# One decoder block on one core: z tiles with meta tokens as two products of 264 columns, one sum of squares over 528 columns, and another order at the start

## The reference, cut to what matters

```
h = concatenate([meta_tokens, x])            # (528, 1024)
y = h * rsqrt(mean(h * h, axis=-1) + 1e-6) * mix_norm_g
z = y @ w_in                                 # 4864 columns: recurrence (q, f, v, gate), attention (q, k, v), branch gates
```

## Time and profile before

| what | us |
|---|---|
| median of 3 runs (1732.18 to 1735.71) | 1732.32 |
| the profiled execution's own time | 1731.5 |
| its span, first to last instruction | 1729.4 |
| PE busy, share of the span | 97% |
| DVE busy | 72% |
| ACT busy | 40% |
| POOL busy | 36% |

### The profile page before, as it was taken

The page is one execution under the profiler, slowest core; times in us unless marked ns, Lnnn a source line. Parts: engine busy times, 40 slices in busy tenths (PEclk is TensorE's granted clock), DMA queues, the critical chain, the costliest instruction groups (busy, mean ns, idle before and its releaser), DMA issues.

```text
span 1729.4 us, 24964 instructions
## 1 busy us (share of the span) xinstructions
PE 1681.4 (97%) x9279; PEld 1477.5 (85%) x9279; DVE 1243.9 (72%) x2191; ACT 688.2 (40%) x978; POOL 628.1 (36%) x420
## 2 busy tenths in 40 slices
PE   7999999999999999999999999999999999999997
PEld 4788866777889999999999999999999999998886
DVE  2550468581688979996877777777777777777875
ACT  4322244543333447775333333333333333333333
POOL 3656233445334542221543343333333333332210
PEclk9999999999999999999999999999999999999999
DMA  3222111143222336678988888888888888888873
GB/s 117 81 73 97 38 49 49 57 151 110 76 83 82 126 122 198 211 208 270 345 304 311 314 298 320 306 293 326 303 301 313 305 316 298 315 278 297 314 258 121
DMA packets 140950, 364.83 MB, mean 211 GB/s; under 512 B 10576, under 2 KB 59728, under 8 KB 140880
## 3 DMA queue, kind: packets, MB, share of 16 engines
q1 hardware_dynamic: 54000, 201.96, 32.7%
q0 software_dynamic: 36864, 134.23, 22.5%
q10 hardware_dynamic: 50016, 27.79, 5.4%
HBM read 336.68 MB, written 27.26 MB: 210 GB/s over the span
## 4 chain that ended last, share of the span: by engine, by line
PE 77%; DVE 14%; issue 3%; ACT 2%; POOL 2%; DMA 1%; SPq 0%; POOLq 0%; ACTq 0%; DVEq 0%
PE ps L1213 71%; DVE hot_g L1150 3%; DVE hot_g L1153 3%; DVE hot_i L1151 3%; PE ps L1279 2%; PE ps L1338 1%; DVE orstd L951 1%; DMA raw<-in_wstream 1%; ACT atp L588 1%; DVE o_hg L952 1%; PE ps L1538 1%; POOL wlo L413 0%; DVE atstat L923 0%; DVE atsc L919 0%; PE ps L1240 0%
## 5 line engine op out<-in xcount | busy, mean ns | idle before, releaser
L1213 PE MATMUL ps<-hThi,uwhi 128*128 128x384 f32 x1024 | 348.6, 340 | 1.8 <-DVE uwlo L1092 1.5
L1213 PE MATMUL ps<-hThi,uwlo 128*128 128x384 f32 x1024 | 344.0, 336 | 0.0
L1213 PE MATMUL ps<-hTlo,uwhi 128*128 128x384 f32 x1024 | 343.1, 335 | 0.0
L1213 PE MATMUL ps<-vwhi,awhi 128*128 128x512 f32 x768 | 299.7, 390 | 3.0 <-DVE awlo L1112 3.0
L1213 PE MATMUL ps<-vwlo,awhi 128*128 128x512 f32 x768 | 299.9, 390 | 0.0
L1213 PE MATMUL ps<-vwhi,awlo 128*128 128x512 f32 x768 | 299.4, 390 | 0.0
L1097 DVE TENSOR_TENSOR vwlo<-vraw,vwhi 128x1024 fp32r<-128x1024 f32 x128 | 156.8, 1225 | 174.5 <-ACT vwhi L719 174.4
L413 POOL TENSOR_TENSOR wlo<-raw,whi 128x1024 fp32r<-128x1024 f32 x66 | 163.4, 2476 | 297.3 <-ACT whi L505 297.3
L719 ACT ACTIVATE vwhi<-vraw 128x1024 fp32r<-128x1024 f32 x128 | 135.8, 1061 | 336.0 <-PE ps L1213 311.3
L468 POOL DMA_INDIRECT rows<-in_u,gidx x128 | 166.6, 1302 | 267.5 <-DVE rows L1120 248.9
L468 POOL DMA_INDIRECT rows<-in_v,gidx x128 | 145.5, 1137 | 297.0 <-DVE acc L1127 279.4
(11 more groups left out here) (292 smaller groups left out, 2820.5 us busy)
## 6 DMA issues: line engine op xcount, KB each, us to landing
uraw<-in_uT SPq DMA_DIRECT2D x128, 512.0 KB, 4.6
vraw<-in_v SPq DMA_DIRECT2D x128, 512.0 KB, 4.7
raw<-in_wstream SPq DMA_DIRECT2D x72, 512.0 KB, 3.2
gates_dram<-piece ACTq DMA_DIRECT2D x12, 2048.0 KB, 9.4
gmat<-gates_dram SPq DMA_DIRECT2D x32, 768.0 KB, 7.6
xt<-in_xT SPq DMA_DIRECT2D x8, 264.0 KB, 6.4
acc<-in_x ACTq DMA_DIRECT2D x1, 2048.0 KB, 11.2
rows<-in_u,gidx POOLq DMA_INDIRECT x128, 6.0
```

Source lines behind the costliest of these rows:

```text
L1213: ins = pe.matmul(dst, lhs[a], rhs[b], start=first and i == 0, stop=last and i == 2)
```

## The change

Tiles with meta tokens become 48 products of 264 columns (two halves of the 528 tokens in two PSUM banks), with the same stationary weights for both halves; the separate meta products, `znat`, its copies and `turn_meta` go. The squares are made after all of y, DVE adds the 8 chunks, and PE multiplies the one sum by ones (2 products of 264 columns) after tile 1. Root and reciprocal are taken over 528 columns. At the start the first 256 columns of tile 0's weights are loaded first and by themselves, then `xt` chunk 0, and `sinks` last; a small ACT copy stands ahead of everything. POOL splits tile 2's weights before it waits for `rstd`, and tile 3's after the scale of tile 0. v and av of the meta tokens are turned in the transposing steps, of which there are 12, with 2 gate products each.

```diff
-TURNED = 10
+TURNED = 12
+SPAN = LEN // 2
+EARLY = 2 * P
...
-            sp.dma_start(par[:], params).then_inc(S["par_in"], 16)
-            sp.dma_start(sink[:], sinks.to_broadcast([P, AQ])).then_inc(S["par_in"], 16)
-            sp.dma_start(raw[:, 0, :], wstream[0]).then_inc(w_in[0], 16)
-            for c in range(DC):
+            sp.dma_start(raw[:, 0, 0:EARLY], wstream[0, :, 0:EARLY]).then_inc(S["early_in"], 16)
+            sp.dma_start(xt[:, 0, :], xT[:, 0, :]).then_inc(xt_in[0], 16)
+            sp.dma_start(par[:], params).then_inc(S["par_in"], 16)
+            sp.dma_start(raw[:, 0, EARLY:D], wstream[0, :, EARLY:D]).then_inc(w_in[0], 16)
+            for c in range(1, DC):
                 sp.dma_start(xt[:, c, :], xT[:, c, :]).then_inc(xt_in[c], 16)
-                if c == 1:
-                    sp.dma_start(raw[:, c, :], wstream[c]).then_inc(w_in[c], 16)
+                if c == 3:
+                    sp.dma_start(raw[:, 1, :], wstream[1]).then_inc(w_in[1], 16)
+            sp.dma_start(sink[:], sinks.to_broadcast([P, AQ])).then_inc(S["sink_in"], 16)
...
+            split_lo(2, 0, slot(0))
             pool.wait_ge(S["rstd_ok"], 1)
-            scale_blocks(0, 4, zm[:, :, META:LEN], 0, "z_copied", "z_out")
+            for k in range(2):
+                if k == 1:
+                    split_lo(3, 1, slot(1))
+                pool.wait_ge(S["z_copied"], k + 1)
+                own = zm[:, k:k + 1, :]
+                pool.tensor_tensor(own, own, rstd[:].unsqueeze(1), ALU.mult).then_inc(S["z_out"], 1)
+            scale_blocks(2, 4, zm, 0, "z_copied", "z_out")
...
+            act.wait_ge(poo, 1)
+            act.activation(rstd[:, 0:1], eps[:], ACT.Copy)
+            act.wait_ge(S["early_in"], 16)
+            act.activation(w["hi"][:, 0, 0:EARLY], raw[:, 0, 0:EARLY], ACT.Copy).then_inc(S["early_hi"], 1)
+            act.wait_ge(S["par_in"], 16)
             for c in range(DC):
                 act.wait_ge(xt_in[c], 16)
                 act.activation(y["hi"][:, c, :], xt[:, c, :], ACT.Copy, scale=mix_g[:, c:c + 1]).then_inc(S["yhi_ok"], 1)
+                if c == 0:
+                    act.wait_ge(w_in[0], 16)
+                    act.activation(w["hi"][:, 0, EARLY:D], raw[:, 0, EARLY:D], ACT.Copy).then_inc(S["w_hi"], 1)
+                if c == 3:
+                    split_hi(1, 1)
+            for c in range(DC):
                 act.activation(xsq[:, c, :], xt[:, c, :], ACT.Square).then_inc(S["xsq_ok"], 1)
+            act.wait_ge(S["w_used"], 1)
+            act.activation(spans(zm[:, 0]), ps[:, 0:2, 0:SPAN], ACT.Copy).then_inc(S["z_copied"], 1)
+            split_hi(2, 0)
+            act.wait_ge(S["w_used"], 2)
+            act.activation(spans(zm[:, 1]), ps[:, 4:6, 0:SPAN], ACT.Copy).then_inc(S["z_copied"], 1)
+            split_hi(3, 1)
             act.wait_ge(S["xsum_ok"], 1)
-            act.activation(sd[:], ps[:, 4, :], ACT.Sqrt, bias=eps[:], scale=1.0 / D).then_inc(S["sd_ok"], 1)
+            act.activation(spans(sd[:]), ps[:, 6:8, 0:SPAN], ACT.Sqrt, bias=eps[:], scale=1.0 / D).then_inc(S["sd_ok"], 1)
...
+            for c in range(1, DC):
+                dve.wait_ge(S["xsq_ok"], c + 1)
+                need(dve, S["xadd_ok"], c - 1)
+                dve.tensor_tensor(xsq[:, 0, :], xsq[:, 0, :], xsq[:, c, :], ALU.add).then_inc(S["xadd_ok"], 1)
...
+            def with_meta(k, c):
+                for i, (a, b) in enumerate(SPLIT):
+                    for n, own in enumerate(halves):
+                        ins = pe.matmul(ps[:, 4 * k + n, 0:SPAN], w[a][:, k, c * P:(c + 1) * P], y[b][:, c, own],
+                                        start=c == 0 and i == 0, stop=c == DC - 1 and i == 2)
+                return ins
...
+            pe.wait_ge(S["early_lo"], 1)
+            for c in range(DC):
+                pe.wait_ge(S["y_ok"], c + 1)
+                if c * P == EARLY:
+                    pe.wait_ge(S["w_lo"], 1)
+                ins = with_meta(0, c)
+            ins.then_inc(S["w_used"], 1)
+            pe.wait_ge(S["w_lo"], 2)
+            for c in range(DC):
+                ins = with_meta(1, c)
+            ins.then_inc(S["w_used"], 1)
+            pe.wait_ge(S["consts"], 1)
+            pe.wait_ge(S["xadd_ok"], DC - 1)
+            for n, own in enumerate(halves):
+                ins = pe.matmul(ps[:, 6 + n, 0:SPAN], ones[:], xsq[:, 0, own], start=True, stop=True)
+            ins.then_inc(S["xsum_ok"], 1)
```

More of the change, by code:

```diff
@@ L196, in build @@
         vnat = at("vnat", [P, TT, 512], F32, X + 12288)
-        znat = at("znat", [META, Z_META, P], F32, X + 20480)
-        vmeta = znat[:, 4:8, :].rearrange("p h d -> p (h d)")
-        avmeta = znat[:, 9, :]
+        vmeta = at("vmeta", [META, 512], F32, X + 20480)
+        avmeta = at("avmeta", [META, P], F32, X + 22528)
         kmeta = at("kmeta", [META, 512], F32, X + 25600)
@@ L485, in transposed_dst @@
                 return avnat[:].rearrange("p t c -> p (t c)")
-            return knat[:, n - 5, :] if n < 9 else kmeta[:]
+            return knat[:, n - 5, :] if n < 9 else (kmeta, vmeta, avmeta)[n - 9][:]
         def transposed_src(n):
@@ L518, in _, with z_pair @@
-            act.activation(meta_sd[:, 0:1], ps[0:META, 5, 0:1], ACT.Sqrt, bias=eps[0:META], scale=1.0 / D
-                           ).then_inc(S["sd_ok"], 1)
+            act.activation(spans(sd[:]), ps[:, 6:8, 0:SPAN], ACT.Sqrt, bias=eps[:], scale=1.0 / D).then_inc(S["sd_ok"], 1)
             act.wait_ge(S["lb_max"], 1)
             act.activation(lbw[:, 3:5], lbw[:, 1:3], ACT.Exp).then_inc(S["lb_exp"], 1)
+            def z_pair(it, dst, shift, meta):
+                for k in range(2):
+                    own = bass.ds(it * 2 + (k - shift), 1)
+                    act.wait_ge(S["w_used"], it * 2 + (k + 1))
+                    if meta:
+                        act.activation(dst[:, own, :].rearrange("p o (b x) -> p (o b) x", b=2), ps[:, 4 * k:4 * k + 2, 0:SPAN], ACT.Copy
+                                       ).then_inc(S["z_copied"], 1)
+                    else:
+                        act.activation(dst[:, own, :], ps[:, 4 * k:4 * k + 1, :], ACT.Copy).then_inc(S["z_copied"], 1)
+                    split_hi(it * 2 + (k + 2), k)
@@ L524, in z_tiles @@
             def z_tiles(first, last, dst, shift, meta):
                 with act.Fori(first // 2, last // 2, 1) as it:
[L526 to L534, removed]
+                    z_pair(it, dst, shift, meta)
@@ L540, in gate_out @@
                 split_hi(T_GATE + t + 2, t % 2)
[L542 to L548, removed]
+            z_pair(1, zm, 0, True)
             act.wait_ge(S["z_out"], 4)
@@ L552, in _ @@
             z_tiles(8, 14, zm, 4, True)
-            act.wait_ge(S["mt_mm"], 2)
-            act.activation(ak_z[:, 0:META], ps[:, 5, 0:META], ACT.Copy).then_inc(S["mt_out"], 1)
             z_tiles(14, N_Z, zr, 10, False)
-            for n in range(1, 10, 2):
+            for n in range(1, TURNED, 2):
                 act.wait_ge(S["tr_mm"], n + 1)
@@ L874, in _ @@
             ins.then_inc(S["hg_ok"], 1)
-            for n in range(0, 10, 2):
+            for n in range(0, TURNED, 2):
                 dve.wait_ge(S["tr_mm"], n + 1)
@@ L1224, in project, with z_pair @@
                 return ins
-            def z_pair(it, meta=None):
+            halves = [slice(b * SPAN, (b + 1) * SPAN) for b in range(2)]
+            def with_meta(k, c):
[4 more added lines that the diff above has]
+                return ins
+            def z_pair(it, meta):
                 for k in range(2):
@@ L1231, in z_pair @@
                     need(pe, S["z_copied"], it * 2 + (k - 1))
-                    if isinstance(it, int) and it == k == 0:
-                        pe.wait_ge(S["consts"], 1)
+                    if meta:
                         for c in range(DC):
[L1236 to L1243, removed]
-                    else:
-                        ins = project(k, y, ps[:, k, :])
@@ L1246, in z_pair @@
[L1246 to L1250, removed]
-                    ins.then_inc(S["w_used"], 1)
[L1253 to L1262, removed]
+                            ins = with_meta(k, c)
+                    else:
+                        ins = project(k, y, ps[:, 4 * k, :])
+                    ins.then_inc(S["w_used"], 1)
+            pe.wait_ge(S["early_lo"], 1)
[4 more added lines that the diff above has]
+                ins = with_meta(0, c)
@@ L1294, in _ @@
                     srcs = [av_z[:, tile(tt)] for tt in range(TT)]
+                elif n < 10:
+                    srcs = [kk[:, h, tile(n - 5) if n < 9 else slice(0, META)] for h in range(HH)]
                 else:
-                    srcs = [kk[:, h, tile(n - 5) if n < 9 else slice(0, META)] for h in range(HH)]
+                    srcs = [v_z[:, h, 0:META] for h in range(HH)] if n == 10 else [av_z[:, 0:META]]
                 rows = P if n < 9 else META
@@ L1302, in _ @@
             for k in ("tr_out_v", "tr_out_s"):
[L1303 removed]
```

(1 more changed line is left out.)

49 lines of the change are left out of this document (25 added, 24 removed).

## The result

The changed kernel takes 1718.72 us (median of 4 executions, 1714.94 to 1719.7), the kernel before 1733.74 beside it. The ratio is 0.9909, with an interval of 0.9889 to 0.9929: faster by 0.9%. Forecast were 1710.8 and a range to 1717, so the direction was right and the size was not: 15.0 us were gained of a forecast 21.5. A second series of the changed kernel gave 1718.72 again (5 executions, ratio 0.9913, 0.9899 to 0.9926).

A forecast was written before the change was run, and what follows sets the result against it. PE was taken as the bound (77% of the chain). Gains of 13.0 (start), 8.0 (tiles 8 to 13) and 1.0 (wait and transposes), less 0.6 (transposing), sum to 21.4: 1731.5 becomes 1710.1, the median 1710.8 us; range 1706.5 to 1717.

The forecast's parts named there:

- the wait before tile 3: PE idle 4.6 us between tiles 2 and 3, while POOL scales tile 0 before it splits tile 3.
- rival 1: The clock falls in PE's idle time before tile 3, costing 3 us, for 1713.8 us; chance 0.25.
- a shift of the transposing stage should stand at the end unchanged: Behind the z tiles nothing has a fixed time, so the gain of 21.4 us up to there reaches the end.
- T1: End of tile 1 on PE, forecast at 21.4 us, with PE starting near 6.1 and tile 0 ending at 15.6.
- Products of 264 columns: PE's products in meta tiles take 0.1195 us each with hidden weight loads; a tile takes 5.74 instead of 7.08 us.
- The row group rule: Rival for meta tiles: weight loads add to products, 0.23 us each, 1758 us in all; chance 0.03.
- From T1 to tile 3: Root, reciprocal, POOL's scale of tile 0, then its split of tile 3: tile 3 starts at T1 + 11.3 us.
- Tile 3 to the sigmoid: After tile 3: ACT copy, POOL split and scale, then ACT's table load 5.7 us after tile 3's end, at 44.1.
- Tile 8: Tile 8 starts 13.0 us earlier, at 64.8, since the sigmoid and DVE's row move with the start.
- Transposing stage: The stage gets two more steps and a last ACT copy: 0.6 us more, bounds 0 and 1.2.

The follow-up runs named there:

- e_fill: Changed kernel plus six unread products of 264 columns behind tile 2, in TensorE's wait before tile 3; 1714.06 us, ratio 0.9887.
- ctl_after: The changed kernel with no edit, run again; 1718.72 us.
- e_split3_dve1: e_split3 with tile 1 split by DVE instead of POOL, between chunks 3 and 4 of y's lo part; 1710.55 us, ratio 0.987.
- ctl_before: The kernel before the change with no edit, run again; 1733.59 us over 12 executions, ratio 0.9996.
- e_warm: Changed kernel plus nine products of ones by ones (128 columns) ahead of the first real product; 1720.74 us, ratio 0.9925.
- e_split3: Changed kernel with POOL's split of tile 3 moved ahead of its wait for the reciprocal; 1713.54 us, ratio 0.9883.
- e_fill_all: Changed kernel plus filling products before tile 3, ahead of tile 8 and ahead of the last two v blocks; 1713.46 us, ratio 0.9885.

## Why the prediction was wrong

Two steps of the sum failed, and both took TensorE's clock to stay at full rate. The first is the wait before tile 3: the forecast counted it for its length alone and left the fall of the clock to rival 1, at 0.25. It fell in both profiled executions of the changed kernel, and e_fill shows that this costs 2.7 to 2.8 us. The second is "a shift of the transposing stage should stand at the end unchanged": 4.7 us of it were lost behind that stage, 3.9 of them at two later falls. A smaller one is T1, the end of tile 1, which came 2.1 us late. The order of waits around the root and the price of the products were right.

By its own steps, against the profiled execution of after:

- **Products of 264 columns**: forecast 0.1195, measured 0.122 (35.14/288). Right in kind; the weight loads hide. The row group rule of the Trainium skill ("TensorE: Matmul & The Clock Gate", Part 3, "The mechanism") does not hold here: load and product would be 0.23 apart by it. The same section also names a background weight buffer as a way for a load to go ahead of running products, and the measured 0.122 is in line with that. The miss is 0.12 a tile, 0.7 us over tiles 8 to 13. The trace of before held a nearer row than the ones that I used: 96 products of 256 columns with weights of 128, from 435.4 to 449.0, are 0.12 apart.
- **T1, the end of tile 1**: forecast 21.4, measured 23.5 here and 25.4 in ctl_after. I had PE busy from 6.1 on without a wait, and tile 0 ending at 15.6; it ended at 17.6. PE started 0.5 later, since `yhi` 0 waited for the DMA of `par`. It then waited twice for lo parts of y, 2.3 us together, and won 0.7 back because the clock rose at 13.0 and not at 14. The wait of 1.12 before chunk 4 is POOL's split beside DVE, which I had not seen; e_split3_dve1 shows it, since there that wait is gone. The wait of 1.16 before chunk 1 is another matter: POOL does nothing then, and e_split3_dve1 still has it (1.27). In after DVE makes `ylo` 1 only behind its split of the rest of tile 0's weights (7.33 to 8.29), and ACT makes `yhi` 1 only at 7.79; my sum had no wait for it. In ctl_after the two waits are the same (2.3 us) and the clock rose only at 18.8; tile 1 ends 2 us later. I had bounded the end of tile 0 at 16.7, too narrowly for both.
- **From T1 to tile 3**: forecast 11.3, measured 34.48 - 23.5 = 11.0. The chain root, reciprocal, scale, split was right in each link, and so was what PE waits for. The wait was 3.0 us and not 4.6, since the additions (1.08 and not 0.7 each) made tile 2 late. In ctl_after, where tile 1 was later, they were done in time, and the wait was 4.1.
- **The clock in that wait**: this was rival 1. I had tied it to the length of the wait: 3.0 us had let the clock stand in my one execution of before, and 4.6 was to be longer than that. It fell in a wait of 2.96 us. ctl_before shows it falling in the very wait in which it had stood, at 1714.4 (3.03 us there), and e_warm shows it standing in the wait before tile 3. So at these lengths the same wait can go either way, and one profiled execution cannot tell that it is harmless. A chance of 0.25 was too low: eight of the nine executions of the changed kernel took over 1718 us, the other one 1714.94.
- **Tile 3 to the sigmoid**: forecast 7.0 from tile 3's end, measured 48.59 - 43.03 = 5.6. The table load, formerly behind the wait for POOL, now lies ahead of it, at 44.81. A gain of 1.4 us that I missed. The change also takes away an earlier wait of ACT there (`mt_out`); that this is why the load moved is my reading, and no run isolates it.
- **Tile 8** comes at 67.92 and not 64.8: the terms are +2.1 (T1), -0.3 (T1 to tile 3), +2.8 (clock and pitch in tile 3) and -1.4 (to the sigmoid), 3.2 together, against the 3.1 by which it is late.
- **Transposing stage**: 147.57 to 158.27 is 10.70 and was 10.19; 0.5 more against 0.6 forecast. Up to here the changed kernel is 17.8 us ahead, of 21.4 forecast.
- **From there to the end** I had the shift unchanged. The span is only 13.1 shorter: 4.7 us are lost behind 158 us. Both traces have the same 8410 products there, so they can be set side by side one by one. The lead of the changed kernel is 17.8 us until the fall at 258.8, which costs 1.5 but is won back by 280 (17.6). The fall at 299.7 takes it to 15.0, for good. At 798 it drops to 14.5 without a fall, where PE's wait for `uwlo` (shown below) is 2.0 us instead of 1.5. It is still 14.5 at 1699, and the fall there leaves 13.1. So the falls are worth 2.6 and 1.3 us, the longer wait 0.5, and why it is longer is open. Such falls come without the change as well: ctl_before has two. Whether the change makes them more frequent, no run tells. My profiled execution of before had none, the median that I started from, 1732.32, was 1.2 below that of all 47 executions of before (1733.5), and the range held nothing for falls behind the z tiles.

The wait for `uwlo` in before, and then in after (total us, times, longest):

```profile
PE ps L1213 <- DVE uwlo L1092: 1.5, 1, 1.5
```

```profile
PE ps L1241 <- DVE uwlo L1120: 2.0, 1, 2.0
```

Of the 8.3 us between the forecast span (1708.0) and the measured one (1716.3), 3.6 arise up to the end of the transposing stage, with the fall before tile 3 as the greatest part, and 4.7 behind it. That the range was missed by only 1.7 us owes something to luck: the sigmoid's unforeseen 1.4 us offset part of the errors.

## What to carry to other kernels

Where an engine order makes TensorE wait for a few microseconds, price the wait twice: for itself and for the half rate behind it; and get several executions with their granted clock before calling a wait harmless. When work is moved beside other work, look at whether the two engines stop each other: here a POOL split of 2.4 us cost DVE 1.7 to 2.0 us. And when a chain is taken off one tile, ask at once what the next tile in the same order waits for; moving one more split moved the median by 5.2 us, where the first one was worth 3.5.

## What the runs showed of the hardware

The clock fell in or right behind waits of 1.94 us (e_split3), 2.09 us (e_warm), 2.96 us (after), 3.03 us (ctl_before) and 4.08 us (ctl_after), and stood in others of 1.91 (after), 2.93 (e_warm) and 3.0 us (the profiled execution of before); the same program differs from execution to execution. In the attention stage it also fell where no wait is longer than 1.2 us (at 299.7 in after). With the wait before tile 3 filled by six products whose result nobody reads (0.47 us each), it stood in both traces, e_fill and e_fill_all. DVE's operations with two inputs took 0.70 us alone and 1.12 on average with POOL's 2.4 us subtraction beside them, four of them losing 1.7 us; seven additions lost 2.0 us to another one (7.58 against 5.58). Products of 264 columns with weights of 128 columns were 0.122 us apart.
